# The first norm's gain: from a transfer to every partition to one row spread by TensorE, with token tile 0 loaded in two halves

## The reference

```python
def rms_norm(x, g):
    xf = x.astype(jnp.float32)
    y = xf * lax.rsqrt(jnp.mean(xf * xf, axis=-1, keepdims=True) + EPS)
    return (y * g.astype(jnp.float32)).astype(x.dtype)

for layer in range(DEPTH):                       # DEPTH = 2
    h = rms_norm(x, g_mix[layer])                # x (1, 256, 1024), g_mix (2, 1024)
    proj = h @ w_in[layer]                       # (1024 x 5648), split into ten parts
    y_a = mla_branch(...); y_b = gla_branch(...); y_c = pool_branch(...)
    ...                                          # gates, merge, output projection
    x = x + merged @ w_out[layer]
    h = rms_norm(x, g_ffn[layer])
    x = x + (swiglu(h, ...) if layer % 2 == 0 else moe_ffn(h, ...))   # moe: 8 experts, top 2
```

## Time and profile before

| what | value |
|---|---|
| median of 3 runs | 1094.86 us (1094.3 to 1095.23) |
| the profiled execution: time | 1095.56 us |
| the profiled execution: span of the trace | 1093.5 us |
| TensorE busy, matmuls | 1077.9 us, 99% of the span |
| VectorE busy | 834.2 us, 76% |
| ScalarE busy | 680.6 us, 62% |
| moved by the DMA engines | 250.21 MB, mean 229 GB/s |

### The profile page before, as it was taken

One profiled execution on the slowest core, in us unless ns is written; L12 is line 12 of the kernel. 1 busy time (PEld: TensorE's weight loads), 2 busy tenths in 40 slices (PEclk: granted clock), 3 DMA queues, 4 the chain that ended last, 5 costly groups with the idle time before them and its releaser, 6 DMA issues.

```text
span 1093.5 us, 17054 instructions
## 1 busy us (share of the span) xinstructions
PE 1077.9 (99%) x6583; PEld 927.5 (85%) x6583; DVE 834.2 (76%) x1159; ACT 680.6 (62%) x966; POOL 73.3 (7%) x119
## 2 busy tenths in 40 slices
PE   9999999999999999999999999999999999999997
PEld 6979888889999998979788877888888888888885
DVE  5678766986555557567966787899899898989896
ACT  5676756455344534657665646876767677777763
POOL 5002430000000000000612000000000000000000
PEclk9999999999999999999999999999999999999999
DMA  9553444567456445355354546899999899999992
GB/s 281 166 164 116 153 156 155 161 240 267 149 173 225 159 169 162 107 155 179 101 166 143 177 163 238 264 356 324 336 330 373 293 359 326 383 325 363 344 351 104
DMA packets 147703, 250.21 MB, mean 229 GB/s; under 512 B 5198, under 2 KB 108708, under 8 KB 147620
## 3 DMA queue, kind: packets, MB, share of 16 engines
q1 hardware_dynamic: 145840, 246.89, 66.3%
q10 hardware_dynamic: 1780, 2.19, 0.6%
HBM read 248.02 MB, written 1.05 MB: 228 GB/s over the span
## 4 chain that ended last, share of the span: by engine, by line
PE 89%; DVE 7%; DMA 1%; ACT 1%; issue 1%; DVEq 0%; ACTq 0%
PE PS L689 27%; PE PS L1229 11%; PE PS L1230 11%; PE PS L1231 11%; PE PS L1027 6%; PE PS L1028 6%; PE PS L1026 6%; PE PS L787 2%; DVE m_lo L1983 2%; PE PS L713 2%; PE PS L887 1%; DMA ring<-in_w_exp_up_dram 1%; PE PS L1178 1%; PE PS L1166 1%; DVE scr L2265 1%
## 5 line engine op out<-in xcount | busy, mean ns | idle before, releaser
L446 DVE TENSOR_TENSOR w_lo<-ring,w_hi 128x1536 fp32r<-128x1536 f32 (+1 forms) x192 | 311.0, 1632 | 97.6 <-ACT w_hi L437 97.3
L437 ACT ACTIVATE w_hi<-ring 128x1536 fp32r<-128x1536 f32 (+1 forms) x192 | 264.6, 1387 | 121.8 <-PE PS L1028 71.8
L1983 DVE TENSOR_TENSOR m_lo<-ring,m_hi 128x512 fp32r<-128x512 f32 (+2 forms) x256 | 183.5, 745 | 68.5 <-ACT m_hi L1456 66.3
L1456 ACT ACTIVATE m_hi<-ring 128x512 fp32r<-128x512 f32 (+2 forms) x256 | 157.7, 631 | 122.5 <-PE PS L689 121.1
L689 PE MATMUL PS<-m_hi,h_hi 128*128 128x512 f32 (+2 forms) x352 | 125.7, 357 | 0.7 <-DVE m_lo L1983 0.7
L1229 PE MATMUL PS<-w_hi,hTe 128*96 128x384 f32 (+1 forms) x384 | 125.1, 326 | 0.0
L1230 PE MATMUL PS<-w_hi,hTe 128*96 128x384 f32 (+1 forms) x384 | 123.9, 323 | 0.0
L1231 PE MATMUL PS<-w_lo,hTe 128*96 128x384 f32 (+1 forms) x384 | 123.7, 322 | 0.0
L689 PE MATMUL PS<-m_hi,h_lo 128*128 128x512 f32 (+2 forms) x352 | 120.6, 343 | 0.0
L689 PE MATMUL PS<-m_lo,h_hi 128*128 128x512 f32 (+2 forms) x352 | 120.5, 342 | 0.0
L1026 PE MATMUL PS<-h_hi,w_hi 128*128 128x256 f32 x352 | 99.9, 284 | 0.0
(11 more groups left out here) (351 smaller groups left out, 2207.6 us busy)
## 6 DMA issues: line engine op xcount, KB each, us to landing
ring<-in_w_in_dram SPq DMA_DIRECT2D x39, 1024.0 KB, 5.2
ring<-in_w_exp_gate_dram SPq DMA_DIRECT2D x24, 1536.0 KB, 7.9
ring<-in_w_exp_up_dram SPq DMA_DIRECT2D x24, 1536.0 KB, 9.9
ring<-in_w_exp_down_dram SPq DMA_DIRECT2D x24, 1536.0 KB, 8.9
ring<-in_w_branch_dram SPq DMA_DIRECT2D x12, 1024.0 KB, 5.1
ring<-in_w_ffn_gate_dram SPq DMA_DIRECT2D x6, 1536.0 KB, 6.9
ring<-in_w_ffn_up_dram SPq DMA_DIRECT2D x6, 1536.0 KB, 6.6
ring<-in_w_ffn_down_dram SPq DMA_DIRECT2D x6, 1536.0 KB, 6.5
```

The costliest lines, as they stand in the source:

```text
L437: act.activation(split_parts(u, j)[0], ring[:, i % NSLOT, w0:w0 + words], ACT.Copy)\
L446: dve.tensor_tensor(lo, ring[:, (j // 2) % NSLOT, w0:w0 + words], hi.bitcast(F32), SUB).then_inc(sem(f"lo_ready{b}"), 1)
L1456: act.activation(hi, raw, ACT.Copy).then_inc(sem("m_hi_ready"), 1)
L1983: dve.tensor_tensor(lo, raw, hi.bitcast(F32), SUB).then_inc(sem("m_lo_ready"), 1)
```

## The change

The gain of the first norm is no longer written to all partitions by the transfer. ACT's transfer brings the row of 1024 to partition 0 alone. TensorE then makes two matrix products in plain float32, with a one-row block of `ones` (1 x 128) and 512 columns of the row each, into the banks 6 and 7; all 128 partitions of a bank hold the same half row afterwards. One signal, `first_gain`, is raised by the second product. For the first norm DVE reads the gain from these banks. For the later norms everything is as before.

Token tile 0 comes in two transfers of 128 x 512 instead of one of 128 x 1024, each with a semaphore of its own. DVE's first product waits for the left half, its second one for the right half. ACT's squares of token tile 0, much later, wait for both.

```diff
         def _(sp):
             x_rows = A["x"].rearrange("b (a p) d -> p (b a) d", p=P)
-            sp.dma_start(x_tok[:, 0, :], x_rows[:, 0, :]).then_inc(sem("x_in0"), 16)
+            for c in range(2):
+                sp.dma_start(x_tok[:, 0, c * 512:(c + 1) * 512], x_rows[:, 0, c * 512:(c + 1) * 512])\
+                  .then_inc(sem(("x_in0", "x_in0b")[c]), 16)
...
             zeros(FIRST_ZEROS, IDLE_BANK)
             pe.wait_ge(sem("ident_ready"), 1)
+            pe.wait_ge(sem("gain_in"), 16)
+            for c in range(2):
+                mm = pe.matmul(PS[:, 6 + c, :], ones[0:1, :], gain[0:1, c * 512:(c + 1) * 512], start=True, stop=True)
+            mm.then_inc(sem("first_gain"), 1)
...
-            act.dma_start(gain, A["g_mix"][0:1, :].broadcast_to([P, D])).then_inc(sem("gain_in"), 16)
+            act.dma_start(gain[0:1, :], A["g_mix"][0:1, :]).then_inc(sem("gain_in"), 16)
...
                 if w == 0:
                     act.wait_ge(sem(f"x_in{a}"), 16)
+                    if a == 0:
+                        act.wait_ge(sem("x_in0b"), 16)
...
                 dve.wait_ge(sem("gain_in"), 16 * (w + 1))
                 if w == 0:
-                    dve.wait_ge(sem(f"x_in{a}"), 16)
-                dve.tensor_tensor(xn[:, a, d], x_tok[:, a, d], gain[:, d], MUL).then_inc(sem("xn_ready"), 1)
+                    dve.wait_ge(sem("first_gain"), 1)
+                    dve.wait_ge(sem("x_in0b" if (a, c) == (0, 1) else f"x_in{a}"), 16)
+                dve.tensor_tensor(xn[:, a, d], x_tok[:, a, d], gain[:, d] if w else PS[:, 6 + c, :], MUL).then_inc(sem("xn_ready"), 1)
```

## The result

| | before | changed |
|---|---|---|
| median, 16 runs each | 1094.56 us (1093.92 to 1096.20) | 1096.72 us (1096.03 to 1097.78) |
| ratio | | 1.0020, 95% interval 1.0012 to 1.0028 |
| the profiled execution: time, span | 1095.56, 1093.5 us | 1097.78, 1095.7 us |

The changed kernel is 2.2 us slower. The interval excludes no change; whether the loss is over 0.2%, it leaves open.

The account below looks back on a forecast made before the run. The gain's transfer, setting DVE's first product at 6.26 us, was taken as the opening's bound; zero blocks plus the 1.72 us pair move it to 8.39, +2.1 us: profiled 1097.7, median 1097.0 us, range 1095.5 to 1098.4.

Parts of the forecast that it names:

- part 4: From DVE's first product on: gain in PSUM adds nothing, saves at most 0.2 us; ACT's table-load limit vanishes.
- What bounds the opening, and that the rest moves with it: Opening: the gain's transfer sets DVE's first product at 6.26 us; moving that start moves all the rest equally.
- Part 1: Opening transfers: without the 512 KB gain write, token tile 0 lands 1.7 us sooner, at about 4.4 us.
- Part 2: The two products on PE: four records of 0.429 us, 1.72 us for the pair, last one drains 163 ns.
- The bound "nothing is saved": Pair on PE: a single-row operand saves nothing, because the array streams the same 512 columns; 1.72 us taken.
- single-record rival: Pair on PE: one record per product, pair 0.86 us, delay 1.27, time 1096.1 us; chance 0.08.
- Part 3: PE's stream: the pair queues behind 13 zero blocks, starts at 6.49, result at 8.37, DVE at about 8.39 us.
- PE's gap ahead of the turns costs nothing, nothing after it ran slower: PE's wait from 8.37 to about 9.2 us, ahead of the turns, costed at nothing, as a similar earlier gap slowed nothing.
- The clock rival: Opening on PE: the clock's rise comes at another moment, giving 1095.9 us if sooner, 1098.3 if later; chance 0.22.
- the prediction's own signs: Profile after: right if DVE's first product starts at 8.4 us, released by PE; wrong if before 8 us.
- Absorbed: Expert-weight wait of 10.80 us at 726.59 swallows the 2.1 us, leaving 1094.9 or slightly less; chance 0.08.
- The sum: Whole kernel: DVE's start moves from 6.26 to 8.39, 2.13 us later, rounded to +2.1 us; median 1097.0.

Follow-up runs that it names:

- idle one-row pair: Kernel before plus two one-row float32 products behind the 13 zero blocks, results unused; 1094.93 us in one run.
- row-only kernel: Changed kernel with token tile 0 back in one transfer, gain row and pair kept; ratio 1.0021 (1.0013 to 1.0030).
- early pair: Changed kernel with 5 zero blocks ahead of the pair, not 13, and a signal per product: 1.0004; with ACT's table load also moved ahead: 1.0002.
- halves only: Changed kernel with the gain again written to all partitions by the transfer and no pair; token tile 0 stays split; ratio 1.0008 (0.9998 to 1.0018).
- the one with 8 zero blocks: Changed kernel with 128 rows in the pair, 8 zero blocks ahead instead of 13, a signal per product; ratio 1.0014 (1.0005 to 1.0023).

## Why the prediction was right

DVE's timeline, the first `split`, in the kernel before and then in the one with the idle one-row pair (used in part 4):

```profile
9.07 0.90 DVE L1983 TENSOR_TENSOR m_lo<-ring,m_hi 128x512 fp32r<-128x512 f32 x1
```

```profile
9.80 0.68 DVE L1985 TENSOR_TENSOR m_lo<-ring,m_hi 128x512 fp32r<-128x512 f32 x1
```

- **What bounds the opening, and that the rest moves with it**: right. The offset stays between 2.7 and 2.5 us over 700 us of program, and the row-only kernel carries the whole loss.
- **Part 1, the transfers**: right. Token tile 0 lands at 3.5 and 4.7 us (4.4 was forecast for the whole), and it is worth nothing, since DVE waits for PE.
- **Part 2, 1.72 us for the pair**: right for 128 rows, mis-sized by 0.2 us for the pair as it stands in the changed kernel (1.92). The bound "nothing is saved" was not the upper end of the pair's price that it was taken for. The row that it came from is narrow in the columns (128\*16), the pair in the rows (1\*128), so it could not show this. The single-record rival is out: four records everywhere.
- **Part 3, the place in the stream**: right in kind. The first product came at 8.80 instead of 8.39: 0.2 us from the row, 0.15 from zero blocks that ended later (5.73 us instead of 5.58), the rest from the step between PE and DVE (0.08 us, I had taken 0.02). The row was there in time; the early pair started at 3.31, so it landed at most 2.5 us after its issue.
- **Part 4, the relay**: from DVE's first product to the long run of matmuls it took 11.99 us before and 11.63 in the third execution of the changed kernel, 0.36 less. Little of that is the gain in PSUM. DVE's first record is as long as before (689 against 693 ns); from its start to the turns it took 0.84 us with the gain in SBUF (before, halves only) and 0.74 in every kernel with the gain in PSUM and a gap ahead of the turns, 0.10 less, for a reason that stays open. Some 0.2 us more come from another instruction, the first `split` (the rows above): 0.90 us before, and 0.68 in the third execution of the changed kernel. It takes 0.68 in the kernel with the idle one-row pair as well, where the gain is in SBUF, so it is not owed to the changed operand. And the step "PE's gap ahead of the turns costs nothing, nothing after it ran slower" failed: in four of the seven traced executions with one-row products behind 13 zero blocks the clock fell, and the same stretch took 12.06 to 12.51 us, 0.4 to 0.9 more than 11.63. A gap of that size alone did not do it, where the pair had 128 rows; nor did it before, at 9.38 to 10.02, the place that the prediction leaned on. In the medians this step cost nothing that the runs can show.
- **The clock rival**: it was no alternative but a part of the case. The rise came at 6.8, 5.4 and 3.8 us in three executions of one kernel, which moves DVE's start from 8.80 to 7.39. By the prediction's own signs a start before 8 us is one of being wrong, and one of the three executions shows it. Where the gain comes by the large transfer, the wait hides the moment: 6.26 us before and 6.30 in the kernel with the halves only, for rises at 6.4 and 5.3. The Trainium skill, "TensorE: Matmul & The Clock Gate", section "Part 1: The HAM clock gate", says that the number of slow matmuls at a kernel's start varies from run to run; the traces agree, with 4.31 to 5.73 us for the same 13 blocks. The scatter that the prediction drew from it isn't shown: the changed kernel's 16 runs spread over 1.75 us, the 16 before over 2.3, or 1.3 without the slowest.
- **Absorbed**: this rival is out, for the reason given against it; the wait, here of 11.48 us, moved along.
- **The sum**: +2.1 forecast, +2.16 measured. The fit to 0.1 us is in part luck. In the profiled execution the start came 0.41 us later than forecast, and the stretch behind it took 0.14 us more than before (12.13 against 11.99; the fall of the clock outweighed the shorter relay), which makes the offset 2.68. That its time came out at 1097.78 with 1097.7 forecast rests on the long end of the trace of before: DVE's last product was 3.55 us later, not 2.1. In the medians it is not known how the runs' rises lay; the execution of 1094.90, from a later series whose kernel before has a median of 1094.19, lies below all of the 16.

## What to carry to other kernels

Before a wait on a transfer is traded for work on an engine, read what stands ahead of that work in the engine's stream: here the filler that costs nothing while everyone waits for a transfer became the path, and the half tile that arrived 2.6 us sooner waited for it. Taking such filler away was not free here either: with 8 blocks fewer and the one-row pair in their place DVE started 0.8 us before the kernel of before, and the long run of matmuls still began 0.6 and 1.2 us behind it, with a clock that rose at 11.7 and 13.0 us. And ask what hides the moment at which the clock rises: the wait for the transfer did, and without it DVE's start moved by 1.4 us between executions of one kernel.

## What the runs showed of the hardware that was not expected

- Two float32 products of 512 columns with one row in both operands took 1.91 us right behind the zero blocks, with 128 rows 1.72; the first record took 692 against 592 ns, and the first weight load did not run ahead of it. Behind a gap 128 rows were hardly cheaper: from first start to last end 1.95 us, against 1.98 for one row behind the zero blocks, with a first record of 667 ns.
- The profile counts one-row products as busy time of TensorE, but the clock did not behave as with full blocks. It fell in the middle of eight records without a gap (granted 0.50 in 8 to 14 us), fell after the pair and the gap of 0.84 us in three more executions (0.72), and rose only at 11.7 and 13.0 us where such products filled most of the start. It stayed up in three traces with a one-row pair, two of them with no gap ahead of the turns. With 128 rows it never fell (two gaps of 0.78 and 0.84 us included), in three traces.
- The 4 KB row landed within 2.5 us when issued at 0.82. Issued at 1.93, behind the large loads, it took 4.44 us in one kernel and about 3.0 in another (the one with 8 zero blocks, whose pair it released at 5.08).
